# Fifteen pairs of feed-forward tiles behind two plain ones, their activation sums made inside the output projection, and the query turns moved between token tiles

## The reference, cut to what matters

```python
h = rms_norm(x, g_mix); proj = h @ w_in           # queries q_b, keys, values, gates ...
...
x = x + merged @ w_out
h2 = rms_norm(x, g_mlp)
x = x + jnp.square(jax.nn.relu(h2 @ w_ff1)) @ w_ff2   # w_ff1: 1024 x 4096
```

## Time and profile before

| | us |
|---|---|
| median of 3 runs | 753.8 (753.77 to 753.89) |
| profiled execution, its own time | 751.51 |
| its span, first to last instruction | 749.8 |
| TensorE busy | 739.9 (99%) |
| VectorE busy | 512.0 (68%) |
| ScalarE busy | 414.6 (55%) |
| GpSimd busy | 172.6 (23%) |

### The profile page before, as it was taken

The page is one execution under the profiler, slowest core; times in us unless marked ns, Lnnn a source line. Parts: engine busy times, 40 slices in busy tenths (PEclk is TensorE's granted clock), DMA queues, the critical chain, the costliest instruction groups (busy, mean ns, idle before and its releaser), DMA issues.

```text
span 749.8 us, 11767 instructions
## 1 busy us (share of the span) xinstructions
PE 739.9 (99%) x4326; PEld 640.8 (85%) x4326; DVE 512.0 (68%) x970; ACT 414.6 (55%) x775; POOL 172.6 (23%) x188
## 2 busy tenths in 40 slices
PE   9999989999999999999999999999999999999998
PEld 9998977877997878777888799999998888888886
DVE  5478788769986877757656988888875443534443
ACT  7768377756778886654356655665565323223230
POOL 3110336523555544300022132222210000000000
PEclk9999999999999999999999999999999999999999
DMA  9622222101111021112532333333333233332322
GB/s 340 239 80 62 63 85 64 51 29 57 57 57 57 29 80 34 57 57 84 198 113 84 93 105 113 114 95 103 95 104 111 86 104 94 97 101 86 111 85 112
DMA packets 21833, 70.94 MB, mean 95 GB/s; under 512 B 2449, under 2 KB 3601, under 8 KB 21521
## 3 DMA queue, kind: packets, MB, share of 16 engines
q1 hardware_dynamic: 21776, 70.19, 29.0%
HBM read 68.08 MB, written 2.10 MB: 94 GB/s over the span
## 4 chain that ended last, share of the span: by engine, by line
PE 85%; DVE 6%; issue 3%; ACT 3%; POOL 1%; DMA 1%; SPq 0%; DVEq 0%; POOLq 0%
PE psum L1818 23%; PE psum L1820 23%; PE psum L1819 23%; PE psum L1826 5%; PE psum L2005 4%; PE psum L1982 2%; PE psum L1983 2%; ACT w_hi L932 1%; DMA x2T<-in_xT 1%; POOL nrstd L833 1%; DVE cmp_in L1439 1%; DVE x2T L1800 1%; DVE hT_lo L1657 1%; DVE w_lo L1307 1%; DVE x2T L1652 1%
## 5 line engine op out<-in xcount | busy, mean ns | idle before, releaser
L932 ACT ACTIVATE w_hi<-stage 128x512 fp32r<-128x512 f32 (+4 forms) x149 | 119.2, 807 | 121.5 <-DMA stage<-in_panels 113.8
L1307 DVE TENSOR_TENSOR w_lo<-stage,w_hi 128x1024 fp32r<-128x1024 f32 (+4 forms) x78 | 82.1, 1058 | 122.7 <-ACT w_hi L932 122.4
L1818 PE MATMUL psum<-hT_hi,w_hi 128*128 128x512 f32 (+1 forms) x332 | 119.0, 358 | 1.1 <-DVE w_lo L1702 1.1
L1819 PE MATMUL psum<-hT_lo,w_hi 128*128 128x512 f32 (+1 forms) x332 | 113.0, 340 | 0.0
L1818 PE MATMUL psum<-a_hi,w_hi 128*128 128x512 f32 x256 | 99.6, 389 | 0.0
L1819 PE MATMUL psum<-a_lo,w_hi 128*128 128x512 f32 x256 | 99.6, 389 | 0.0
L1820 PE MATMUL psum<-a_hi,w_lo 128*128 128x512 f32 x256 | 99.6, 389 | 0.0
L1820 PE MATMUL psum<-hT_hi,w_lo 128*128 128x512 f32 (+1 forms) x280 | 98.5, 352 | 0.0
L1107 ACT ACTIVATE prob<-prob,neg_max 128x128 f32<-128x128 f32 (+3 forms) x96 | 53.7, 560 | 33.3 <-DVE neg_max L1519 32.5
L896 POOL TENSOR_TENSOR w_lo<-stage,w_hi 128x512 fp32r<-128x512 f32 x46 | 59.6, 1301 | 38.4 <-ACT w_hi L932 38.3
L1818 PEld LDWEIGHTS psum<-hT_hi,w_hi 128*128 128x128 f32 x332 | 63.1, 190 | 5.9 <-DVE w_lo L1702 1.5
(11 more groups left out here) (275 smaller groups left out, 1665.0 us busy)
## 6 DMA issues: line engine op xcount, KB each, us to landing
stage<-in_panels SPq DMA_DIRECT2D x104, 512.0 KB, 3.6
xT_in<-in_xT SPq DMA_DIRECT2D x8, 260.0 KB, 4.7
x_in<-in_x SPq DMA_DIRECT2D x4, 512.0 KB, 7.1
phi<-in_phi SPq DMA_DIRECT2D x2, 1024.0 KB, 6.2
x2T<-in_xT SPq DMA_DIRECT2D x1, 2048.0 KB, 8.5
out_xT<-x2T SPq DMA_DIRECT2D x8, 256.0 KB, 2.0
stage<-in_panels SPq DMA_DIRECT2D x8, 212.0 KB, 4.8
stage<-in_panels SPq DMA_DIRECT2D x4, 408.0 KB, 3.1
```

The lines of the kernel that those rows point to most:

```text
L932: return nc.scalar.activation(dst, src, ACT.Copy, scale=scale)
L1307: tt_op(w_lo[:, p % SLOTS, cols], stage[:, p % SLOTS, cols], hi_place(p)[:, cols].bitcast(F32), ALU.subtract)\
L1818: mm(dst, a_h, b_h, start=start, stop=False)
L1819: mm(dst, a_h, b_l, start=False, stop=False)
```

## The change

It changes the order in three places and the number of pairs:

1. The plain tiles are the first two (`PLAIN = 2`), and 15 pairs follow. The two plain tiles at the end are gone; the second product comes right behind pair 14.
2. `sum_t(i)`, `round_t(i)` and `low_t(i)` now serve the k-blocks 2i and 2i + 1, so each needs only two tiles of the output projection. `sum_t` becomes three VectorE instructions (512, 256 and 256 elements) chained by a semaphore. The first three stand inside the output loop, the fourth behind it.
3. The reciprocal of the norm is taken in four pieces, in pairs 1 to 4. At the end of the pairs VectorE and ScalarE make the activations of tiles 0 to 2 while the last pair runs.
4. The query turns: token tile 0 ahead of `C_KV2`'s third panel, tile 1 behind it, tiles 2 and 3 piece by piece between the token tiles of the fourth panel. `low_q` of tile 0 stands ahead of the wait for Tanh. The rounding and low rest of the last piece move into the script's units 0 and 1.

```diff
-PLAIN_FIRST, PLAIN_LAST = 4, 2
+PLAIN = 2
...
-    late = {1: [("kw_sq",)], ...
+    late = {0: [("qb_hi",)], 1: [("kw_sq",)], ...
-    early = {4: [("kw_dup",)], ...
+    early = {1: [("qb_low",)], 4: [("kw_dup",)], ...
...
-    Y_ORDER = [6, 7, 0, 1, 2, 3, 4, 5]
+    Y_ORDER = [4, 5, 6, 7, 0, 1, 2, 3]
...
 # ScalarE, output loop
             for i in range(KT):
                 wait_drained(se, ("out", i))
                 copy(hT_hi[:, i, :], x2T[:, i, :], ...)
                 ...
                 nc.scalar.activation(sq2[:, i % 2, :], x2T[:, i, :], ACT.Square).then_inc(x2_squared, 1)
-                round_panel(OUT0 + AHEAD + i)
+                if i < KT - 1:
+                    round_panel(OUT0 + AHEAD + i)
                 copy(h2[:, i, :], x2T[:, i, :], ...)
+                if i and i % 2 == 0:
+                    round_t(i // 2 - 1)
...
 # ScalarE, behind it
-            round_panel(FF1 + 3)
             se.wait_ge(x2_added, KT)
             copy(ss_st[:, 0, :], sq2_sum[:, :]).then_inc(ss_hi_done, 1)
-            round_t(0)
-            round_t(1)
+            round_t(3)
+            round_s12(0)
             square_u(0)
             round_first(0)
-            round_t(2)
-            round_t(3)
-            square_u(1)
-            square_u(2)
-            round_s12(0)
             round_s34(0)
...
 # VectorE
+            def sum_t(i):
+                ve.wait_ge(h2_done, 2 * i + 2)
+                t, flat = t_sum[i], h2[:, 2 * i:2 * i + 2, :]
+                tt_op(t[:, 0::2, :], flat[:, :, S // 2:], flat[:, 0, :].rearrange("p (a t) -> p a t", a=2), ALU.subtract)\
+                    .then_inc(t_chain, 1)
+                ve.wait_ge(t_chain, 2 * i + 1)
+                tt_op(t[:, 1, :], flat[:, 1, S // 2:], t[:, 0, :], ALU.subtract).then_inc(t_chain, 1)
+                ve.wait_ge(t_chain, 2 * i + 2)
+                tt_op(t[:, 3, :], flat[:, 1, 0:S // 2], t[:, 1, :], ALU.subtract).then_inc(t_summed, 1)
...
             for i in range(KT):                       # output loop: x2T, split_panel, hT_lo, then
+                if i and i % 2 == 0:
+                    sum_t(i // 2 - 1)
+                elif i >= 3:
+                    low_t((i - 3) // 2)
-            split_panel(OUT0 + AHEAD + KT - 1)
...
-            split_panel(FF1 + 3)
-            ve.wait_ge(h2_done, KT)
-            sum_t(0, ...) ... sum_t(3, ...)           # four of 1024 elements
             ve.wait_ge(ss_hi_done, 1)
             tt_op(ss_st[:, 1, :], ...)                # ss_lo
-            for i in range(4):
-                low_t(i)
-            ps = wait_full(ve, "ss")
-            ...
-            link(nc.vector.reciprocal(rstd_bc[:, :], rstd_bc[:, :]))
+            sum_t(3)
             sum_s12(0)
+            low_t(3)
             low_first(0)
...
                 sum_5(n)
+                if n == 0:
+                    ps = wait_full(ve, "ss")
+                    ...
+                elif n <= TT:
+                    r = rstd_bc[:, (n - 1) * P:n * P]
+                    link(nc.vector.reciprocal(r, r))
                 if n + 1 < PAIRS:
                     low_s(n + 1, 0)
                     low_s(n + 1, 1)
                 else:
-                    split_panel(FF1 + LAST + 1)
-                    split_panel(FF2)
-            scale_act(0)
+                    scale_act(1)
+                    split_act(0)
+                    split_panel(FF2 + 1)
+                    scale_act(2)
+                    split_act(1)
+                    split_panel(FF2 + 2)
+                    split_act(2)
             sum_34(PAIRS - 1)
...
 # TensorE
-            for tt in range(TT):
-                te.wait_ge(qb_normed, tt + 1)
-                ... both halves; behind tile 1: proj(C_KV2, 2), gelT
-            proj(C_KV2, 3)
+            turn_qb(0)
+            proj(C_KV2, 2)
+            turn_qb(1)
+            proj(C_KV2, 3, tts=range(0, 2))
+            te.wait_ge(ev["gelu"], 1)
+            transposes("gelT", [gel[:, :]])
+            turn_qb(2, [0])
+            proj(C_KV2, 3, tts=[2])
+            turn_qb(2, [1])
+            turn_qb(3, [0])
+            proj(C_KV2, 3, tts=[3])
+            turn_qb(3, [1])
```

More of the change, by code:

```diff
@@ L315, in hybrid_layer @@
     B_SS = 7
[L316 to L319, removed]
-    Y_ORDER = [6, 7, 0, 1, 2, 3, 4, 5]
+    PAIRS = (NFF - PLAIN) // 2
+    assert FF1 % SLOTS == 0 and FF2 % SLOTS == 0 and PLAIN == 2 and PAIRS % 2
+    Y_ORDER = [4, 5, 6, 7, 0, 1, 2, 3]
     bank = Banks()
@@ L363, in hybrid_layer @@
         bank.use(("out", i), i % FF1_BANKS)
-    for f in range(PLAIN_FIRST):
+    for f in range(PLAIN):
         bank.use(("ff1", f), (f + KT) % FF1_BANKS)
@@ L400, in hybrid_layer @@
     for f in range(NFF):
-        if f in PLAIN:
+        if f < PLAIN:
             released[FF1 + f] = ("full", ("ff1", f))
         else:
-            released[FF1 + f] = ("full", ("pair", (f - PLAIN_FIRST) // 2, 3 * (f % 2)))
+            released[FF1 + f] = ("full", ("pair", (f - PLAIN) // 2, 3 * (f % 2)))
         released[FF2 + f] = ("used", n_used + f + 1)
@@ L715, in hi_place @@
         def hi_place(p):
-            return w_hi[:, (p + (2 if p >= FF1 + LAST else 0)) % SLOTS, :]
+            return w_hi[:, HI_ORDER[p % SLOTS] if p >= FF2 else p % SLOTS, :]
         def wait_loaded(eng, p):
@@ L1177, in _, with round_t @@
                         copy(mT_hi[:, i, :], merge[0][i][:, :]).then_inc(m_hi_done, 1)
+            def round_t(i):
+                se.wait_ge(t_summed, i + 1)
+                copy(t_hi[i][:, :, :], t_sum[i][:, :, :]).then_inc(t_hi_done, 1)
             for i in range(KT):
@@ L1198, in round_act @@
                 copy(a_hi[:, q % SLOTS, :], act[:, q, :]).then_inc(a_hi_done, 1)
[L1200 to L1202 removed]
             def round_first(n):
[L1206 removed]
+                p = FF1 + PLAIN + 2 * n
                 wait_loaded(se, p)
@@ L1266, in _ @@
                 else:
-                    square_u(3)
+                    square_u(1)
                 take_prod1(n)
@@ L1671, in split_act @@
                     .then_inc(a_lo_done, 1)
-            even, odd = [h2[:, i::2, :] for i in range(2)]
             first, second = slice(0, S // 2), slice(S // 2, S)
[L1677 to L1683, removed]
-                tt_op(t_lo[t][:, :, :], t_sum[t][:, :, :], t_hi[t][:, :, :].bitcast(F32), ALU.subtract)\
-                    .then_inc(t_lo_done, 1)
             def sum_s12(n):
                 (a11, _), (a21, a22), _, _ = pair_panels(n)
-                p = FF1 + PLAIN_FIRST + 2 * n
+                p = FF1 + PLAIN + 2 * n
                 wait_loaded(ve, p)
@@ L1861, in proj @@
                 if i == 3:
-                    turns = [(kk, tt) for tt in range(TT) for kk in range(2)]
+                    turns = [(kk, tt) for tt in tts for kk in range(2)]
                 if p == 0:
@@ L2137, in block_product, with tokens @@
                     cols = slice(k * P, (k + 1) * P)
-                    last = product(dst, a_h[:, cols], a_l[:, cols], b_h[:, k, :], b_l[:, k, :], start=k == 0,
+                    last = product(dst, a_h[:, cols], a_l[:, cols], b_h[k], b_l[k], start=k == 0,
                                    stop=k == KT // 2 - 1)
                 return last
-            even, odd = [(hT_hi[:, i::2, :], hT_lo[:, i::2, :]) for i in range(2)]
-            t = [(t_hi[i], t_lo[i]) for i in range(4)]
+            def tokens(odd, tok):
+                return [[h[:, 2 * k + odd, tok] for k in range(KT // 2)] for h in (hT_hi, hT_lo)]
+            t = [[[part[k][:, i, :] for k in range(KT // 2)] for part in (t_hi, t_lo)] for i in range(4)]
             for n in range(PAIRS):
                 _, _, (a11_lo, a12_lo), (_, a22_lo) = pair_panels(n)
-                block = [w_hi[:, i // 2, i % 2 * SLOT // 2:(i % 2 + 1) * SLOT // 2] for i in range(7)]
+                block = [w_hi[:, i // 2, i % 2 * SLOT // 2:(i % 2 + 1) * SLOT // 2] for i in (0, 1, 4, 5, 6, 7, 2)]
                 s = s_lo[n % 2]
```

178 lines of the change are left out of this document (89 added, 89 removed).

## The result

The changed kernel takes 759.84 us (median of 4 runs, 759.43 to 760.68), where before takes 753.85 beside it (753.77 to 754.02): ratio 1.0081, 95% interval 1.0063 to 1.0098. It is slower by 6.0 us; 760.0 was forecast, and the range and the likeliest case hold it. The profiled execution of after took 760.68, its span is 758.9.

What follows compares the result with a forecast made beforehand. TensorE, busy in 99% of the span, was taken to bound the kernel. Terms 5.7 + 0.3 + 0.2 + 0.4 - 1.2 + 0.8 = +6.2 us on the median 753.8 gave 760.0, range 757.0 to 762.5.

Steps and rivals of the forecast that it cites:

- turns 6.5: Output loop, x2T to x2T: a turn grows from 5.00 to about 6.5 us from turn 2 on.
- the stop at 409: Output loop: TensorE stops 3.2 us in a plain tile, waiting for the second feed-forward panel, split late.
- the first scores at 98.6: Query turns: the waits between token tiles go, so TensorE's first scores can start at 98.6.
- end of the pairs: Behind the last pair: activations no longer hidden by two plain tiles, +0.4 us (bounds 0 and 1.5).
- seam, with contention: Output projection to pairs: +5.7 us from pair work and new waiting, +0.3 from GpSimd and VectorE running at once.
- reciprocals in pairs: Pairs 1 to 4: a quarter of the reciprocal, about 0.85 us, in each; +0.2 us.
- queries: Query turns: -1.2 us (bounds 0 and -3.7), what TensorE can keep by the 1.27 us slack at unit 6.
- clock: Pair 0 after a 5.8 us pause: TensorE comes back slow, +0.8 us (bounds 0 and 2.7).
- nothing can bring pair 0 forward but a shorter ring: Seam: claimed that only a shorter output-loop turn of VectorE and ScalarE could start pair 0 sooner.
- the ring: Output loop: VectorE and ScalarE wait on each other; work added behind `hT_lo` delays the last x2T by 7.5 us.
- The ring has room: Rival, output loop: sums cost under 0.46 us per turn, total 749.8 us; 5%.
- The query gain goes through whole: Rival, query turns: -3.7 instead of -1.2 us and no slow clock, total 756.7 us; 15%.

Runs made afterwards that it cites:

- e7: The changed kernel with GpSimd's first weight sum of the first pair put behind VectorE's `sum_s12(0)`: 758.92 us, ratio 1.0062.
- e2: The changed kernel with 46 unread matmuls of 256 columns keeping TensorE busy ahead of the first pair: 757.80 us, ratio 1.0054.
- e1: The kernel before, unchanged, profiled once more: 753.93 us.
- e4: The kernel before with only the change's query turns, GELU order and two late pieces: 751.66 us, ratio 0.9976.
- e9: The changed kernel with the output loop's `sum_t` and `low_t` moved right behind `x2T`, into VectorE's wait: 748.92 us, ratio 0.9940.
- e11: e6 with the activation sums in the output loop moved right behind `x2T`: 747.64 us, ratio 0.9919.
- e6: e4 with 14 pairs behind four plain tiles, none at the end, quartered reciprocal, the change's pair end and in-loop sums: 752.93 us, ratio 0.9987.
- e10: e9 with `sum_t(3)` ahead of `ss_lo` on VectorE and `round_first(0)` ahead of `square_u(0)` on ScalarE: 747.70 us, ratio 0.9918.
- e8: e7 with `square_u(0)` behind `round_first(0)` on ScalarE and 34 idle matmuls in TensorE's wait: 756.80 us, ratio 1.0042.
- e3: The changed kernel with all four activation sums, their roundings and low rests behind the output loop: 757.18 us, ratio 1.0043.

## Why the prediction was right, and where it was not

At the seam the mechanism was right, and most of its places to 0.3 us: turns 6.5 (measured 6.49), last x2T at 412.9 in after's time (412.89), the stop at 409 of 3.2 us (2.96), the first scores at 98.6 (98.29), the end of the pairs +0.4 (the second product starts 0.39 us behind the last pair's end at 580.98). Two terms were too small, and the total came out right because the profiled base lacked 2.3 us that the median has. From profile to profile the second product starts 8.97 us later, 581.37 against 572.4:

| term | forecast | measured |
|---|---|---|
| seam, with contention | +5.7 + 0.3 | +6.9 |
| reciprocals in pairs | +0.2 | +0.1 |
| end of the pairs | +0.4 | +0.4 |
| queries | -1.2 | -1.1 |
| clock | +0.8 | +2.7 |
| sum | +6.2 | +9.0 |

*The seam.* The first pair starts at 426.94; without the query gain of 1.09 it would be 428.03, which is 1.2 behind the forecast's 426.8, 0.9 behind with its own +0.3. All of it stands already at the end of `ss_lo`: 419.46, where the forecast's 419.2 is 418.1 in after's time. The term that was mis-sized is contention. I took the 0.17 by which one panel's split was longer in the earlier trace rows as the size of a collision. It is the size of a small overlap: GpSimd's addition ended 0.3 us into that split. When both engines are issued together the later one waits for the whole of the other's instruction, 1.1 us each time: in after twice (`t_lo`, `ss_lo`), and e7 gave one of them back, 1.11 in the trace. So "nothing can bring pair 0 forward but a shorter ring" was wrong: e7 did it with the ring as it was. In the trace of before GpSimd was the later one at this seam and took 2.31 us (1.29 elsewhere), where nobody waited for it.

*The clock.* The range ran to 2.7, and 2.7 was right for the profile (2.0 in the medians, e2). I valued a stop of 5.8 us by the four matmuls of the earlier trace rows, but the low level lasted from 422.7 to 433, 6 us of it under matmuls, which costs 2.7. By the Trainium skill, page "TensorE: Matmul & The Clock Gate", section "What's actually happening", sustained work must come first before the full clock is back; the trace agrees (work again from 426.94, the full level from 433). The upper bound was the better estimate for a stop of this length.

*The reciprocals.* Each quarter took 0.94 us, and of the pairs behind the first only pair 6 was longer than 10.09, by 0.1. The slack of 1.1 us in the earlier trace rows was larger than one quarter, so hardly anything got through.

*The queries.* The -1.2 came true as -1.1, but not for the reason given. VectorE around the units 2 and 3, before, then after, and a wait of TensorE behind them:

```profile
105.86 0.69 DVE L1316 TENSOR_REDUCE nss<-square_late 128x8 f32<-128x512 f32 x1 [0.46 <-ACT square_late L946]
106.58 0.89 DVE L1318 TENSOR_SCALAR nvar<-nss 128x8 f32<-128x8 f32 x1
107.39 0.28 DVE L1511 TENSOR_TENSOR prob<-psum,dist 128x128 f32<-128x128 f32 x1
...
105.52 0.68 DVE L1319 TENSOR_REDUCE nss<-square_late 128x8 f32<-128x512 f32 x1
106.23 0.17 DVE L1321 TENSOR_SCALAR nvar<-nss 128x8 f32<-128x8 f32 x1
106.31 0.28 DVE L1516 TENSOR_TENSOR prob<-psum,dist 128x128 f32<-128x128 f32 x1
...
122.97 0.66 PE L1837 MATMUL psum<-ident,fac 128*128 128x128 f32 x4 [0.83 <-POOL fac L887]
```

VectorE takes up its old order 0.2 us late, as foreseen (104.97 against 104.78), but at the next unit's scores it is 1.08 ahead: it no longer waits for ScalarE, and `nvar` takes 0.17 instead of 0.89 (in before GpSimd's split of a panel runs until 107.44, in after GpSimd is idle then). TensorE kept more than the slack of unit 6, 2.28 us there, and lost all but 1.1 at 122.97. The 1.1 that go through are the size of VectorE's lead, which the forecast doesn't have. That the number fits is luck.

*The base.* I took the difference of 2.3 us between the profiled execution and the median as a constant. Against e1 it was the absence of two events: a clock fall in the query turns (1.2) and a collision at the seam (1.2). The change takes away the first (e4: 2.15 us gained where 1.2 was forecast) and replaces the seam in which the second stood. So between these two profiles the change costs 9.2 us (760.68 - 751.51), between medians 6.0. Against e1's trace, which has both events, the terms are: seam +5.7, queries -2.3, clock +2.7, reciprocals and end of the pairs +0.5, in all +6.5 (581.37 - 574.83; the rest is rounding). There the seam fits the forecast's 6.0, and what cancels is 1.1 too little for the queries against 1.9 too little for the clock. The forecast of +6.2 missed 3.0 of the 9.2, and the two profiled executions stood 2.3 under and 0.8 over their medians, 3.2 together. The errors cancelled; the ring and the stops were foreseen, but that the total was met to 0.2 us is luck.

*The rivals.* "The ring has room" was refused for this kernel, yet e9 shows that the ring had it: I wrote that VectorE's idle 2.33 us "doesn't help, as it works in order". True for that order. The same four lines one place earlier are hidden whole, and the time lands at 748.9, near that rival's 749.8. "The query gain goes through whole" fails in the profile: of the 4.05 us lead at the first scores 1.09 is left.

## What to carry to other kernels

When work is put into a loop in which two engines hand to and fro, its price is decided by the side of the wait on which it stands: behind the wait it lengthens each turn by its whole length, inside it by nothing (e9 against after: 10.9 us; e11 against e6: 5.3). Before one sums up from one profiled execution that is shorter than the median, one finds out which event it lacks, for a change may act on just that. Cover given away (plain tiles) is to be held against all work of the other engines behind the last point at which they can start, not against the work moved.

## What the hardware showed that was not expected

- VectorE and GpSimd, both reading SBUF, ran one after the other: 1.22 became 2.31, 0.69 became 1.78 (after), 0.68 became 1.57 and 0.42 became 1.40 (e10, `sum_t(3)` beside GpSimd's sums). GpSimd's 1.26 became 2.27 in its turn. A VectorE instruction with one small operand was held too: `nvar`, 128 x 8, took 0.89 and 0.88 beside GpSimd's work (before, e1) and 0.17 without (after, e4).
- The granted clock falls in some executions and not in others on the same schedule: with equal waits in the query turns it went to 0.50 in e1 and not in the first profile (29 of the 36 runs of before have the mean clock of e1 or a lower one, where they fell is not known); after a stop of 3 us at 409 it stayed at 1.00 in after, e2, e6 and e7 and fell in e8:

```profile
410.00:412.00 2.00, 1.16 (x5) 0.99 (x6) 2.00 (x3) 0.00 (x0) 0.00 (x0) 1.00 0.00 0
412.00:414.00 2.00, 2.00 (x7) 1.58 (x6) 1.49 (x4) 1.00 (x2) 0.00 (x0) 0.56 0.00 0
414.00:416.00 2.00, 2.00 (x7) 1.55 (x7) 1.23 (x2) 1.80 (x4) 0.73 (x1) 0.58 0.00 0
```

  All runs of e8 had 0.998. In e2 and e6, where both clocks occurred, the runs with 0.998 were no longer than those with 1.000, in e6 even shorter (752.2 to 752.5, against 753.0 to 753.7). In e8's trace the fall lies ahead of waits that take it up; why runs with a fall are shorter in e6, no run tells. Behind each stop over 6 us that was left idle (after 6.69, e3 7.28, e7 6.23) it fell. What decides for the shorter ones is open; no run here tells it.
